# RWKV loop: preparation of one chunk in every iteration, and inversion levels over all eight head pairs at once

## The reference, cut to what matters

```python
def step(S, inp):
    r_t, w_t, k_t, v_t, kk_t, b_t = inp
    sa = jnp.einsum('bhvk,bhk->bhv', S, kk_t)
    S = (S * w_t[:, :, None, :] - sa[..., None] * b_t[:, :, None, :]
         + v_t[..., None] * k_t[:, :, None, :])
    return S, jnp.einsum('bhvk,bhk->bhv', S, r_t)
```

## Time and profile before

| | |
|---|---|
| median of 3 runs | 2999.66 us (2999.21 to 3003.76) |
| the profiled execution | 3002.31 us |
| its span in the trace | 3000.5 us, mean granted TensorE clock 0.943 |
| PE busy over the span | 2717.9 us |
| the phase `rwkv_loop` in the trace | 2030.09 us (first matmul) to 2418.21 us |
| the same for PE | busy 299.05 us of 388.12 us |

### The profile page before, as it was taken

How to read it: one execution, slowest core, us unless ns; L and a number is a source line. 1 busy time by engine, 2 the same in 40 slices (tenths; PEclk the granted TensorE clock), 3 DMA queues, 4 the chain that set the end, 5 groups by cost and what they waited for, 6 DMA issues and landing times.

```text
span 3000.5 us, 46544 instructions
## 1 busy us (share of the span) xinstructions
PE 2717.9 (91%) x20206; PEld 1974.1 (66%) x20206; DVE 1418.4 (47%) x2486; ACT 516.1 (17%) x1033; POOL 162.8 (5%) x112
## 2 busy tenths in 40 slices
PE   7989999998999898999999988997778769999996
PEld 3643788886645445888884743546777733788885
DVE  3153655525004436555424365254444463877624
ACT  2121100001013322000001032013333211122100
POOL 0000000000000000000000000003333200000000
PEclk9979999999998989999999977997999979999998
DMA  5313222233120002232234101200000013222231
GB/s 189 97 36 98 71 85 85 67 100 100 57 84 1 1 30 83 93 96 84 58 99 128 42 15 56 56 1 2 4 4 4 4 57 98 71 85 84 67 91 53
DMA packets 219563, 190.34 MB, mean 63 GB/s; under 512 B 8667, under 2 KB 216956, under 8 KB 219360
## 3 DMA queue, kind: packets, MB, share of 16 engines
q1 hardware_dynamic: 219066, 187.27, 20.2%
q10 hardware_dynamic: 294, 0.09, 0.0%
HBM read 185.25 MB, written 2.10 MB: 62 GB/s over the span
## 4 chain that ended last, share of the span: by engine, by line
PE 81%; DVE 12%; issue 2%; ACT 2%; DVEq 0%; DMA 0%; POOLq 0%; POOL 0%; ACTq 0%; SPq 0%
PE psum L1138 26%; PE psum L335 18%; PE psum L1348 13%; PE psum L365 4%; PE psum L2041 4%; PE psum L2048 3%; PE psum L778 2%; PE psum L800 2%; DVE sbuf L277 1%; PE psum L786 1%; PE psum L776 1%; DVE sbuf L290 1%; PE psum L2118 1%; PE psum L1751 1%; DVE sbuf L2431 1%
## 5 line engine op out<-in xcount | busy, mean ns | idle before, releaser
L1138 PE MATMUL psum<-sbuf 128*128 128x256 f32 x3696 | 810.6, 383 | 9.9 <-DVE sbuf L1197 6.5
L1138 PEld LDWEIGHTS psum<-sbuf 128*128 128x128 f32 x3696 | 708.7, 192 | 110.8 <-DVE sbuf L1197 7.7
L335 PE MATMUL psum<-sbuf 128*128 128x512 f32 (+5 forms) x1424 | 542.4, 543 | 22.7 <-DVEq L434 22.5
L335 PEld LDWEIGHTS psum<-sbuf 128*128 128x128 f32 (+3 forms) x1424 | 264.5, 187 | 295.8 <-issue 257.1
L1348 PE MATMUL psum<-sbuf 128*128 128x256 f32 x1848 | 405.2, 382 | 12.4 <-DVE sbuf L1365 6.8
L1348 PEld LDWEIGHTS psum<-sbuf 128*128 128x128 f32 x1848 | 353.8, 192 | 63.5 <-DVE sbuf L1365 7.6
L1222 DVE TENSOR_TENSOR sbuf<-sbuf,psum 128x256 f32<-128x256 f32 x462 | 177.7, 415 | 205.7 <-PE psum L1138 204.5
L2048 PE MATMUL psum<-sbuf 64*64 64x64 f32 x4992 | 204.8, 232 | 32.6 <-issue 19.1
L2041 PE MATMUL psum<-sbuf 64*64 64x64 f32 (+1 forms) x4544 | 180.0, 233 | 50.3 <-DVE sbuf L2409 30.6
L2048 PEld LDWEIGHTS psum<-sbuf 64*64 64x64 f32 x4992 | 180.0, 143 | 44.2 <-issue 38.1
L2041 PEld LDWEIGHTS psum<-sbuf 64*64 64x64 f32 x4544 | 164.5, 141 | 57.1 <-DVE sbuf L2409 32.0
(11 more groups left out here) (232 smaller groups left out, 2516.7 us busy)
## 6 DMA issues: line engine op xcount, KB each, us to landing
sbuf<-in_w_mod_dram SPq DMA_DIRECT2D x24, 1024.0 KB, 5.2
sbuf<-in_w_ffn_gate_dram SPq DMA_DIRECT2D x22, 1024.0 KB, 5.5
sbuf<-in_w_ffn_up_dram SPq DMA_DIRECT2D x22, 1024.0 KB, 7.3
sbuf<-in_w_ffn_down_dram SPq DMA_DIRECT2D x32, 704.0 KB, 6.2
sbuf<-in_w_up_dram SPq DMA_DIRECT2D x22, 1024.0 KB, 5.4
sbuf<-in_w_out_dram SPq DMA_DIRECT2D x12, 1024.0 KB, 5.2
sbuf<-in_w_in_dram SPq DMA_DIRECT2D x12, 1024.0 KB, 5.3
sbuf<-in_w_down_dram SPq DMA_DIRECT2D x16, 704.0 KB, 6.3
```

Of the source, the lines that this page charges most:

```text
L335: mm = pe.matmul(bank, w[:, q, c0:c0 + m], rhs(k0 + q), start=start and q == 0, stop=stop and q == kc - 1)
L1138: mm = pe.matmul(bank, w[:, q, :], rhs[:, q, :], start=q == 0, stop=q == 3)
```

## The change

Preparation is per chunk and no longer per block. `latents(c)`, `rate(c)`, `cums(c)` and `exps(c)` treat both directions of one chunk, in level 3 and level 4 of every iteration, for chunk c = n+3; the loop therefore starts at n = -3. The tiles AR, B, K and GAM have four buffers of one chunk in place of two of two chunks. `products(c)` on DVE is a generator (c = n+2): its instructions are handed out behind the updates, five at level 0, two at level 1 and one at each later level.

Each level is done for all 8 pairs at once. T goes to PSUM bank 0, the update of Y to bank 1 and that of X to bank 2. One T copy of 512 columns on ACT stands where two of 256 stood, and one update of 1024 columns on DVE (512 at the last level) where there were two of 512 (256).

```diff
-        def latents(b, d):
-            tok = block_tokens(b, d)
-            pe.matmul(k.bank[4], WA[0:33, tok], W2A[0:33, d, :], start=True, stop=True)
-            for f in range(4):
-                mm = pe.matmul(k.bank[5][:, f * P:(f + 1) * P], W2A[64:97, d, f * P:(f + 1) * P], WA[64:97, tok],
-                               start=True, stop=True)
+        def latents(c):
+            if c >= 1:
+                wait("exps", c)
...
+            for d in range(2):
+                pe.matmul(k.bank[4][HEADS[d], :], WA[0:33, chunk_tokens(c, d)], W2A[0:33, d, :], start=True, stop=True)
+            for d in range(2):
+                for f in range(4):
+                    mm = pe.matmul(k.bank[5][:, column(4 * d + f)], W2A[64:97, d, f * P:(f + 1) * P], WA[64:97, chunk_tokens(c, d)],
+                                   start=True, stop=True)
             mm.then_inc(sems["latent_done"], 1)
...
-            wait("prods", prep(g // 2, 1))
+            wait("prods", g + 1)
...
         def t_level(n, lv, aside):
-            for d in range(2):
-                if d == 0:
-                    wait("loff", LEVELS * n + lv + 1)
...
-                for p in range(4 * d, 4 * d + 4):
-                    mm = crosswise(pe, k.bank[2 * d][:, column(p % 4)], LOFF[lv][:, p, :], X[n % 2][:, p, :])
-                    if p % 4 == 3:
-                        mm.then_inc(sems["t_done"], 1)
-                    next(aside, None)
+            wait("loff", whole(n, lv))
+            if lv == 0:
+                wait("eye", n + 1)
+                if n >= 1:
+                    wait("xy", whole(n - 1, LEVELS - 1))
+            else:
+                wait("xy", whole(n, lv - 1))
+            for p in range(8):
+                mm = crosswise(pe, k.bank[0][:, column(p)], LOFF[lv][:, p, :], X[n % 2][:, p, :])
+                if p == 7:
+                    mm.then_inc(sems["t_done"], 1)
+                next(aside, None)
...
-            if rated_in(n - 1) is not None:
-                wait("rated", prep(rated_in(n - 1), 1))
-            elif exps_in(n - 1) is not None:
-                wait("exps", prep(exps_in(n - 1), 1))
-            elif m >= 1 and main(m - 1):
+            wait("exps", min(n + 3, NCH))
+            if m >= 1 and main(m - 1):
                 wait("y_copied", m - NCH_CTX)
...
-        for n in range(-1, NCH + 1):
-            m, g, live = n - 1, n + 1, 0 <= n < NCH
+        nothing = iter(())
+        for n in range(-3, NCH + 1):
+            m, g, live, c = n - 1, n + 1, 0 <= n < NCH, n + 2
+            filler = products(c) if 0 <= c < NCH else nothing
             for lv in range(LEVELS):
...
-                if lv == 0 and n >= 1 and exps_in(n - 1) is not None:
-                    products(exps_in(n - 1), 1)
...
-            if exps_in(n) is not None:
-                products(exps_in(n), 0)
+                for _ in range((5, 2, 1, 1, 1)[lv]):
+                    next(filler, None)
+            for _ in filler:
+                pass
```

More of the change, by code:

```diff
@@ L2087, in chunk_tokens @@
         return slice(t, t + CH)
[L2089 to L2094, removed]
     main = lambda n: n >= NCH_CTX
[L2097 to L2100, removed]
+    whole = lambda n, lv: LEVELS * n + lv + 1
     column = lambda p: slice(p * CH, (p + 1) * CH)
@@ L2112, in latents, with cums @@
             mm.then_inc(sems["latent_done"], 1)
-        def cums(b, d):
-            wait("rated", prep(b, d))
+        def cums(c):
+            wait("rated", c + 1)
             for f in range(4):
                 o = 2048 + 256 * f
-                mm = pe.matmul(k.psum[:, o:o + 256], SIG[d][:, f * P:(f + 1) * P], mask(k, "sums", 0, 256), start=True, stop=True)
+                mm = pe.matmul(k.psum[:, o:o + 256], SIG[:, f * P:(f + 1) * P], mask(k, "sums", 0, 256), start=True, stop=True)
             mm.then_inc(sems["cums_done"], 1)
[L2121 to L2137, removed]
@@ L2315, in tensor @@
                     new_state(m, n)
[L2316 to L2319, removed]
+                if lv == 3 and c < NCH:
+                    latents(c)
     def scalar(k, act):
         wait = lambda name, value: act.wait_ge(sems[name], value)
[L2324 to L2327, removed]
@@ L2350, in scalar @@
         act.activation(WA[0:32, :], WA[0:32, :], ACT.Tanh).then_inc(sems["tanh"], 1)
[L2351 to L2356 removed]
+        for n in range(-3, NCH + 1):
+            m, live, c = n - 1, 0 <= n < NCH, n + 3
             for lv in range(LEVELS):
                 if live:
[L2359 to L2361 removed]
+                    wait("t_done", whole(n, lv))
+                    act.activation(flat(T), k.bank[0], ACT.Copy).then_inc(sems["t_copied"], 1)
                 if lv == 0:
@@ L2483, in loff @@
             if g >= 1:
-                wait("t_done", halves(g - 1, lv, 1))
+                wait("t_done", whole(g - 1, lv))
             pool.tensor_tensor(split(LOFF[lv]), split(GB[g % 2][:, :, 0, :]), both_level(lv), ALU.mult).then_inc(sems["loff"], 1)
@@ L2488, in pool @@
             [P, 2, 4, CH])
-        for d in range(2):
-            kka(0, d)
-        for n in range(-1, NCH):
-            g = n + 1
-            if n >= 1 and exps_in(n - 1) is not None:
-                kka(exps_in(n - 1), 1)
-            if g < NCH:
+        for n in range(-3, NCH):
+            g, c = n + 1, n + 2
+            if 0 <= c < NCH:
+                kka(c)
+            if 0 <= g < NCH:
                 wait("x_init", g + 1)
@@ L2501, in pool @@
                     loff(g, lv)
-            if exps_in(n) is not None:
-                kka(exps_in(n), 0)
     return Phase("rwkv_loop", tensor=tensor, vector=vector, scalar=scalar, pool=pool)
```

202 lines of the change are left out of this document (93 added, 109 removed).

## The result

The changed kernel takes 3042.35 us in the median (3033.87 to 3046.94, 4 runs), the kernel before 3001.26 beside it: a ratio of 1.0135, 95% interval 1.012 to 1.0151. The prediction was 2991 with a range up to 3010. The profiled execution took 3046.94 us, its span is 3045.2 (before 3000.5).

A forecast was written before the change was run, and what follows sets the result against it. PE was taken as nearly the bound, with holes from product waits and instruction issue. Main -1.9, context -6.6, first stretch -3.4, bare +1.55, start -1 and tail +2.4 made -8.9 us: 2991 us, range 2976 to 3010.

The forecast's parts named there:

- Part 1: Products on DVE, spread and made one iteration ahead: PE's product stall, 5.3 us over two main stretches with cums, goes.
- Part 2: Preparation in each iteration: one cums 1.93 us and one latents 1.65 + 0.65, together 4.2 over the bare stretch.
- Part 3: Whole levels: PE waits for updates and T copies, 3.1 us per iteration (context 3.4); half taken, 1.55 and 1.7.
- tail at +2.4: End of the loop: two more iterations without preparation, paying for whole levels, +2.4 us.
- Part 4: Start and end of the loop: start -1 us (up to 4 more or 6 saved), tail +2.4 us.
- main stretches over 33: Sign of being wrong: stretches between two `x_init` in the four-chunk main part exceed 33 us; 31.4 was forecast.
- a last product over 2 us on DVE: Sign of being wrong: the last product of an iteration (L2367) takes more than 2 us on DVE.
- The T copy at 0.60 and the update at 1.22: Expected sign in each level: the T copy on ACT appears as 0.60 us, the update on DVE as about 1.2.
- The levels cost their full price: Rival, all iterations: each pays 3.1 us for whole levels, 18 us more in all, 3009 us; chance 0.22.
- The product behind POOL: Rival, last product on DVE: waits for all five POOL LOFF copies, +14 to +21 us, 3005 to 3012; chance 0.10.
- The table loads: Rival, ACT's two table loads per iteration: if 1.3 us longer, `kv` is 0.5 to 0.7 late nine times, 2997; chance 0.08.

The follow-up runs named there:

- chunk_blocklat: Also called the fast version: changed kernel with half levels, latents for one direction of two chunks per call, and cums as 16 rows of 64x128; 2969.71 us, ratio 0.9895.
- block_whole: The kernel before with whole levels alone (one T copy and one update per level); 3037.46 us, ratio 1.0129.
- the first benchmark: The kernel before with extra matmuls that wait for nothing ahead of its first latents, output overwritten; 552 rows of one form took 16 us at full clock, 0.029 each.

## Why the prediction was wrong, by its own steps

The forecast for the loop was -8.9 us; it came out at +45.8. The 54.7 between them, by stretches of the changed kernel less those forecast: context (123.88 in all, four of 27.8) +12.7; main (134.30, four of 31.4) +8.7; the first stretch (34.72, 25.0) +9.7; the bare one (30.97, 27.2) +3.8; start and second stretch (+8.8 over before, forecast -1) +9.8; tail (+12.4, forecast +2.4) +10.0.

- **Part 1 was right in kind, and too large.** No PE wait on a product after the start. What remains when the two harmful edits are taken back, chunk_blocklat, is 31 us faster than before. Some 9 of these are its quicker cums, and 22 are left. The forecast's own terms without whole levels and without the +0.65 a call make some 33 (an estimate: -8.9 less 18.6 less 5.9). So about a third of this gain didn't come, and no run shows why.
- **Part 2, the latents, failed.** I bounded the doubled rows by nothing and +1.09 and took +0.65; a call costs +1.80 (2.89 against 1.09). I saw 10 rows in 1.09 us and scaled them, and gave as the reason that the widest rows double. Those cost nothing more: four take 0.96 us, side by side. The narrow ones doubled, from 0.94 to 1.93, and no longer run beside the wide ones. The earlier trace rows shows only the first wide row of a call, and I didn't look at how it overlaps the narrow ones: "a full doubling" was not the worst case, losing the overlap was. At half clock a call is 5.1 to 5.6 us, so the start, taken at -1 with bounds of 5, became +9.8 worse.
- **Part 3 was right in kind and mis-sized.** Half of the waits fall on packet holes, as I took it: 21 of 44 us. But 44 us in twelve iterations are 3.7 each, not 3.1, and what packets leave is 2.0. Over the loop I had 18.6 us for whole levels, and they cost 30. The larger error is the **tail at +2.4**: whole levels cost 7 to 13 us there. The last chunk has no `gram_lt`, latents or cums to cover a T copy or an update. That alone isn't the reason, since the whole update without the whole T copy cost the tail nothing (48.01); what I missed are the T copy's waits and, in two of the three tails, the lower clock (0.85 and 0.88; 0.97 in block_whole).
- **Part 4** fell with these two: the terms for start and tail were the least worked out, and they carry 20 of the 55 us.
- **Two of the signs of being wrong came true:** main stretches over 33 (up to 35.19), and a last product over 2 us on DVE. The T copy at 0.60 and the update at 1.22 came as written.
- **The rivals.** "The levels cost their full price" (3009) was the nearest, and still 33 us short; its mechanism was seen, at 30 us. The product behind POOL came in part, and behind another instruction than I named. The first three times that both stood together (2056 to 2117), L2367 took 2.7 us beside POOL's `eye` (L2456, 2.67). PE paid for it most in the first stretch:

```profile
2079.21 2.73 DVE L2367 TENSOR_TENSOR sbuf<-sbuf 128x512 f32<-128x512 f32 x1
2081.86 1.21 DVE L2388 TENSOR_TENSOR sbuf<-sbuf,psum 128x1024 f32<-128x1024 f32 x1
2083.22 0.27 PE L2048 MATMUL psum<-sbuf 64*64 64x64 f32 x2 [2.69 <-DVE sbuf L2388]
```

  The update starts the moment the product ends, PE's wait is 2.69 us instead of some 1.4, and from 2083.3 to 2100 the granted clock is 0.59. Some of the 9.7 us of that stretch belong here; how many, no run shows. Beside the LOFF copies, later, L2367 took 0.70 to 1.73, so DVE did find a gap, as the forecast had it. The table loads, now two per iteration at the same 1283 ns, show in no wait of PE after the start.
- **Not settled:** the clock. The stretches of the changed kernel stand at 0.80 for the first, at 0.89 to 1.00 for the others, and its tail at 0.85, which is 3 to 6 us longer than the other tails with whole levels (59.57 against 54.00 to 56.32). Neither longer latents nor the waits alone brought all of this in the fast version. Nor is it known what the second table load of an iteration costs.

## What to carry to other kernels

Before splitting or narrowing a matmul, look whether its rows start together with others in the trace; the price is then that of the lost overlap, not of the row count. When two half-steps that cover each other become one, price every level, in the last iterations too, where other cover is gone. Two parts of one change can hide what its other parts gain, here 22 us: take them back one at a time.

## What the runs showed of the hardware, unexpected

- Instructions can bound TensorE: 64x64 rows alternating between two array placements ran at 0.016 us a row and then stood 1.4 to 1.9 us for the next packet, 3.75 us per 128 rows.
- Matmuls of 64 rows in the two halves of the array, into two banks, run side by side: 16 rows of 64x128 on 128 columns in 1.09 us, where 8 rows of 128x128 on 256 columns with the same result take 1.92.
- Wide rows of 64 weight columns for the two halves of the output ran side by side (four in 0.96 us, where two of one direction took 0.95 to 1.00), but none ran beside rows of 128 weight columns.
- The granted clock can fall while PE never stops. In the first benchmark, rows of 64x64 on 16 columns, PE busy throughout:

```profile
2060.00:2075.00 15.00, 15.00 (x286) 15.00 (x286) 0.00 (x0) 0.00 (x0) 0.00 (x0) 0.50 0.01 2
```
